# The second feed-forward norm turn of a two-block transformer kernel, taken by token halves around the last down product

## The reference, cut to what matters

```python
    # first block, per layer
        u = causal_dwconv(hn @ w_up[l], conv_w[l], conv_b[l])
        gate, val = jnp.split(u, 2, axis=-1)
        f = (jax.nn.gelu(gate, approximate=True) * val) @ w_down[l]
        h = h + rms_norm(f, ln_ffn_post[l])
    # second block
        h = rms_norm_2(x, norm1[l])
        proj = h @ w_in[l]

def rms_norm(x, g, eps=NORM_EPS):
    x32 = x.astype(jnp.float32)
    y = x32 * lax.rsqrt(jnp.mean(x32 * x32, axis=-1, keepdims=True) + eps)
    return (y * g.astype(jnp.float32)).astype(x.dtype)
```

## Time and profile before

| | us |
|---|---|
| median of 3 runs | 2956.19 (2954.12 to 2957.56) |
| the profiled execution, own time | 2959.0 |
| its span | 2957.2 |
| PE busy | 2835.6 |
| DVE, ACT, POOL busy | 1848.0, 1269.7, 623.0 |

### The profile page before, as it was taken

How to read it: one execution, slowest core, us unless ns; L and a number is a source line. 1 busy time by engine, 2 the same in 40 slices (tenths; PEclk the granted TensorE clock), 3 DMA queues, 4 the chain that set the end, 5 groups by cost and what they waited for, 6 DMA issues and landing times.

```text
span 2957.2 us, 47458 instructions
## 1 busy us (share of the span) xinstructions
PE 2835.6 (96%) x19678; PEld 2274.4 (77%) x19678; DVE 1848.0 (62%) x2351; ACT 1269.7 (43%) x1879; POOL 623.0 (21%) x313
## 2 busy tenths in 40 slices
PE   8999998889899999999899999999899999999999
PEld 6877777777688888788678867766578888888887
DVE  3157778852599999866685554565645766653446
ACT  4145555542554555443543433343433423333334
POOL 4310122221100000254151200000012122245443
PEclk9999999999999999999999999999899999999999
DMA  6443330002423333465544553435544344465664
GB/s 216 151 121 114 110 131 30 27 26 79 143 89 106 102 101 107 155 220 180 175 133 153 164 178 122 129 112 160 192 150 131 115 150 145 150 216 196 211 238 171
DMA packets 306280, 413.79 MB, mean 140 GB/s; under 512 B 13569, under 2 KB 189834, under 8 KB 306066
## 3 DMA queue, kind: packets, MB, share of 16 engines
q1 hardware_dynamic: 291090, 363.56, 38.6%
q10 hardware_dynamic: 14976, 47.19, 4.2%
HBM read 280.64 MB, written 130.06 MB: 139 GB/s over the span
## 4 chain that ended last, share of the span: by engine, by line
PE 80%; DVE 8%; DMA 4%; issue 3%; ACT 3%; SPq 1%; POOL 1%; DVEq 0%; ACTq 0%; POOLq 0%
PE ps L511 17%; PE ps L2767 16%; PE ps L3300 13%; PE ps L3082 10%; PE ps L2124 5%; PE ps L695 4%; PE ps L1544 4%; PE ps L2175 2%; PE ps L2194 2%; DVE cb L3385 2%; PE ps L2152 1%; PE ps L1607 1%; PE ps L2155 1%; DMA kl<-qk_lo 1%; DMA residual<-src 1%
## 5 line engine op out<-in xcount | busy, mean ns | idle before, releaser
L477 POOL TENSOR_TENSOR wl<-wraw,wh 128x1024 fp32r<-128x1024 f32 x62 | 157.4, 2538 | 1103.0 <-ACT wh L472 1093.4
L511 PE MATMUL ps<-xh,wh 128*128 128x512 f32 x752 | 237.9, 398 | 5.2 <-POOL wl L477 2.3
L511 PE MATMUL ps<-xl,wh 128*128 128x512 f32 x752 | 233.3, 392 | 0.0
L511 PE MATMUL ps<-xh,wl 128*128 128x512 f32 x752 | 232.9, 391 | 0.0
L472 ACT ACTIVATE wh<-wraw 128x1024 fp32r<-128x1024 f32 x78 | 82.4, 1056 | 266.0 <-PE ps L511 205.3
L2756 POOL TENSOR_TENSOR h_dl<-h_dr,h_dh 128x1024 fp32r<-128x1024 f32 x36 | 94.7, 2633 | 477.8 <-ACT h_dh L2738 477.6
L511 PEld LDWEIGHTS ps<-xh,wh 128*128 128x128 f32 x752 | 139.6, 189 | 46.7 <-issue 9.0
L2767 PE MATMUL ps<-h_dh,h_fh 128*128 128x512 f32 x448 | 174.8, 390 | 0.7 <-POOL h_dl L2756 0.7
L2767 PE MATMUL ps<-h_dh,h_fl 128*128 128x512 f32 x448 | 174.4, 389 | 0.0
L2767 PE MATMUL ps<-h_dl,h_fh 128*128 128x512 f32 x448 | 174.3, 389 | 0.0
L511 PEld LDWEIGHTS ps<-xl,wh 128*128 128x128 f32 x752 | 142.4, 189 | 30.3
(11 more groups left out here) (507 smaller groups left out, 7634.6 us busy)
## 6 DMA issues: line engine op xcount, KB each, us to landing
h_fr<-act_d SPq DMA_DIRECT2D x60, 512.0 KB, 3.9
act_d<-act SPq DMA_DIRECT2D x16, 1792.0 KB, 6.7
wraw<-in_w_in SPq DMA_DIRECT2D x48, 512.0 KB, 5.0
h_dr<-in_w_down SPq DMA_DIRECT2D x44, 512.0 KB, 4.8
r_raw<-in_w_up SPq DMA_DIRECT2D x38, 512.0 KB, 3.9
residual<-src ACTq DMA_DIRECT2D x32, 512.0 KB, 5.1
w_raw<-in_w_up SPq DMA_DIRECT2D x32, 512.0 KB, 5.1
l_fr<-act_d SPq DMA_DIRECT2D x31, 512.0 KB, 3.9
```

Source lines behind the costliest of these rows:

```text
L477: nc.gpsimd.tensor_tensor(wl[:, s, :, :], wraw[:, s, :, :], wh[:, s, :, :].bitcast(F32), ALU.subtract).then_inc(w_lo, 1)
L511: mm = nc.tensor.matmul(ps[:, bank + h, :], w, x[:, h * HALF:(h + 1) * HALF], start=start and k == 0, stop=stop and k == 2)
```

## The change

Nothing that is computed changes, but the order and the widths do. A token half is 512 tokens (`FIRST`, `SECOND`).

- **Step 2's parts** are made by ACT between the convolution copies of the gate and the value half, by DVE between the taps of the two.
- **P4's homes.** Steps 36 to 41 use three homes of their own in place of four, in memory that the kept weights held. The first three loads wait for P6 and for sums of P7; the loads of 39 to 41 wait for PE's step i-3.
- **Second half.** Its squares and their sum are made around steps 36 and 37 (`second_half_squares_act`, `second_half_sum_dve`), PE's sum lies in the middle of step 37, the root and reciprocal behind, PE's spread in the middle of step 38. Then its eight tiles are normed, rounded, squared and stored in halves (`second_half_dve`, `second_half_act`): tiles 0 and 1 between the parts of steps 39 and 40, tiles 2 and 3 between those of 40 and 41, tiles 4 to 7 behind. Its residual tiles are loaded apart, one of these loads ahead of the load of step 41.
- **PE** multiplies both input units for the second half behind the last down product (`second_half_products`), then for the first half tile by tile (`first_half_units`). The first half's statistics lie in between.
- Residual loads and stores of this turn are 32 of 256 KB in place of 16 of 512 KB.

```diff
             ff1_tap(act, FF_TILES - 1, "g")
+            down_hi_act(act, down1, 2)
             ff1_tap(act, FF_TILES - 1, "v")
-            down_hi_act(act, down1, 2)
...
+            second_half_root_act(act)
+            down_hi_act(act, down1, LAST1 + 3)
+            for kt in (0, 1):
+                second_half_act(act, kt)
+            down_hi_act(act, down1, LAST1 + 4)
+            for kt in (2, 3):
+                second_half_act(act, kt)
+            down_hi_act(act, down1, LAST1 + 5)
+            for kt in (4, 5):
+                second_half_act(act, kt)
+            for m in (4, 5):
+                first_half_squares_act(act, m)
+            second_half_act(act, 6)
+            for m in (6, 7):
+                first_half_squares_act(act, m)
+            stat_root_act(act, 3, ROWS[0], HALF_BANK)
+            second_half_act(act, 7)
+            post_norm_act(act, 1, 16, 32, "norm1_2", FIRST)
...
-                down_products(pe, down1, i)
+                down_products(pe, down1, i, {LAST1 + 1: second_half_sums_pe, LAST1 + 2: second_half_spread_pe}.get(i))
             down_last_products(pe, down1)
-            post_sums_pe(pe, 24, KT - 2)
-            spread_pe(pe, 3)
-            paced_units(pe, U_FA, 0, 16, 32, 4)
+            second_half_products(pe, 0, 1, {2: lambda pe: first_half_sums_pe(pe, 24), 6: first_half_spread_pe})
+            second_half_products(pe, 1, 3, {})
+            first_half_units(pe)
...
+        def second_half_dve(dve, kt):
+            s = kt % 2
+            if kt == 0:
+                h1_pe.wait(dve, "spread", 0)
+            h1_dve.done(nc.vector.tensor_tensor(y[:, kt, SECOND], y[:, kt, SECOND], ps[:, 7, :], ALU.mult), f"m{kt}")
+            h1_dve.wait(dve, f"m{kt}", 0)
+            dve.wait_ge(h_loaded[s], 16 * (4 + kt // 2 + 1))
+            dve.wait_ge(src_stored[s], 16 * ((16 + kt) // 2))
+            h1_dve.done(nc.vector.scalar_tensor_tensor(
+                out=src[:, s, SECOND], in0=y[:, kt, SECOND], scalar=col("ln_ffn_post", kt), in1=hres[:, s, SECOND],
+                op0=ALU.mult, op1=ALU.add), f"r{kt}")
+            h1_act.wait(dve, f"x{kt}", 0)
+            h1_dve.done(nc.vector.scalar_tensor_tensor(
+                out=xl[:, kt, SECOND], in0=src[:, s, SECOND], scalar=col("norm1_2", kt),
+                in1=xh[:, kt, SECOND].bitcast(F32), op0=ALU.mult, op1=ALU.subtract), f"l{kt}")
+
+        def second_half_act(act, kt):
+            tile = src[:, kt % 2, SECOND]
+            h1_dve.wait(act, f"r{kt}", 0)
+            h1_act.done(nc.scalar.activation(xh[:, kt, SECOND], tile, ACT.Identity, scale=col("norm1_2", kt)), f"x{kt}")
+            nc.scalar.activation(y[:, kt, SECOND], tile, ACT.Identity, scale=col("norm1_2", kt))
+            h1_act.done(nc.scalar.activation(sq1[:, kt, FIRST], tile, ACT.Square), f"s{kt}")
+            act.dma_start(residual[kt][:, SECOND], tile).then_inc(src_stored[kt % 2], 16)
+
+        def second_half_products(pe, u, bank, after):
+            for kt in range(KT):
+                h1_dve.wait(pe, f"l{kt}", 0)
+                if u == 0:
+                    h1_act.wait(pe, f"s{kt}", 0)
+                    for q in (2, 3):
+                        mm = nc.tensor.matmul(ps[QUARTERS[q], STAT_BANK, 0:T // 4], ones[:, :],
+                                              sq1[:, kt, (q - 2) * T // 4:(q - 1) * T // 4], start=kt == 0, stop=kt == KT - 1)
+                    h1_pe.done(mm, f"p{kt}")
+...
+                half_tile(bank, u, kt, SECOND)
+                if kt in after:
+                    after[kt](pe)
+
+        def half_tile(bank, u, kt, part):
+            for w, x, k in ((wh, xh, 0), (wh, xl, 1), (wl, xh, 2)):
+                mm = nc.tensor.matmul(ps[:, bank, :], w[:, u, kt, :], x[:, kt, part],
+                                      start=kt == 0 and k == 0, stop=kt == KT - 1 and k == 2)
+            return mm
+
+        def first_half_units(pe):
+            for kt in range(KT):
+                square_sum_pe(pe, 32 + kt, (0, 1))
+...
+                pe.wait_ge(x_lo, 16 + kt + 1)
+                mm = half_tile(0, 0, kt, FIRST)
+                if 1 <= kt < KT - 1:
+                    half_tile(2, 1, kt - 1, FIRST)
+            mm.then_inc(mm_done, 1)
+            half_tile(2, 1, 6, FIRST)
+            spread_pe(pe, 4)
+            half_tile(2, 1, 7, FIRST).then_inc(mm_done, 1)
...
             for i in range(8, len(down1.steps)):
+                if i == LAST1 + 3:
+                    for kt in (0, 1):
+                        second_half_loads(sp, kt)
+                elif i == LAST1 + 5:
+                    second_half_loads(sp, 2)
                 down_load(sp, down1, i)
...
+        LAST1, TURNS = (d.steps.index(("P4", 0)) for d in downs)
```

More of the change, by code:

```diff
@@ L130 @@
     kept2: list
+    last: list
 CHUNK = 64
@@ L568, in spread_pe, with spread_half_pe @@
             mm.then_inc(spread_done, 1)
+        def spread_half_pe(of, half):
+            rows = ROWS[half]
+            for w, part in ((spread_even, 0), (spread_odd, 1)):
+                mm = nc.tensor.matmul(ps[:, 6 + half, part * T // 4:(part + 1) * T // 4], w[rows, :], of[rows, :],
+                                      start=True, stop=True)
+            return mm
         def rstd_copy_act(act, k):
@@ L2567, in build_program @@
         act2_stored = [sem(f"act2_stored{s}") for s in range(2)]
+        h1_act = Steps(sem("h1_act"), [f"q{m}" for m in range(KT)] + ["root"] +
+                       [f"{x}{kt}" for kt in range(KT) for x in "xs"])
+        h1_dve = Steps(sem("h1_dve"), [f"a{m}" for m in range(KT)] + ["rec"] +
+                       [f"{x}{kt}" for kt in range(KT) for x in "mrl"])
+        h1_pe = Steps(sem("h1_pe"), ["sum", "spread"] + [f"p{kt}" for kt in range(KT)])
         s1_dve = Steps(sem("s1_dve"), ["T1", "T3", "T2", "T4"])
@@ L2636, in post_norm_loads, with second_half_squares_act @@
                     sp.wait_ge(added, KT * k + kt - 1)
-                sp.dma_start(hres[:, kt % 2, :], residual[kt]).then_inc(h_loaded[kt % 2], 16)
+                elif k:
+                    h1_dve.wait(sp, f"r{KT - 2 + kt}", 0)
+                sp.dma_start(hres[:, kt % 2, part], residual[kt][:, part]).then_inc(h_loaded[kt % 2], 16)
+        def second_half_squares_act(act, m):
+            if m < 4:
+                act.wait_ge(down_added, down_added_by(down1, "P3", m))
+            else:
+                act.wait_ge(down_added, down_added_by(down1, "P7", m - 4))
+            if m >= 2:
+                h1_dve.wait(act, f"a{m - 2}", 0)
+            h1_act.done(nc.scalar.activation(sq[:, m % 2, SECOND], y[:, m, SECOND], ACT.Square), f"q{m}")
@@ new lines, in second_half_sum_dve, with second_half_sums_pe @@
+        def second_half_sum_dve(dve, m):
+            h1_act.wait(dve, f"q{m}", 0)
+            if m == 0:
+                dve.wait_ge(stat_root, 3)
+                ins = nc.vector.tensor_copy(ss[:, SECOND], sq[:, 0, SECOND])
+            else:
+                h1_dve.wait(dve, f"a{m - 1}", 0)
+                ins = nc.vector.tensor_tensor(ss[:, SECOND], ss[:, SECOND], sq[:, m % 2, SECOND], ALU.add)
+            h1_dve.done(ins, f"a{m}")
+        def second_half_sums_pe(pe):
+            pe.wait_ge(down_added, down_added_by(down1, "P3"))
+            h1_dve.wait(pe, f"a{KT - 1}", 0)
+            h1_pe.done(quarter_sums(ss, True, True, (2, 3)), "sum")
@@ new lines, in second_half_root_act, with second_half_reciprocal_dve, second_half_spread_pe @@
+        def second_half_root_act(act):
+            h1_pe.wait(act, "sum", 0)
+            rows = ROWS[1]
+            h1_act.done(nc.scalar.activation(root1[rows, :], ps[rows, STAT_BANK, 0:T // 4], ACT.Sqrt,
+                                             bias=small[rows, 0:1], scale=1.0 / D), "root")
+        def second_half_reciprocal_dve(dve):
+            h1_act.wait(dve, "root", 0)
+            h1_dve.done(nc.vector.reciprocal(root1[ROWS[1], :], root1[ROWS[1], :]), "rec")
+        def second_half_spread_pe(pe):
+            h1_dve.wait(pe, "rec", 0)
+            h1_pe.done(spread_half_pe(root1, 1), "spread")
@@ L2640, in down_home @@
         def down_home(d, i):
+            name, c = d.steps[i]
+            if name == "P4" and d.last:
+                return d.last[c % 3]
             return (d.later if d.later and i >= 4 else d.homes)[i % 4]
@@ L2781, in down_products @@
             for b in range(4):
+                if b == 2 and half_way is not None:
+                    half_way(pe)
                 if c == 0 and name in DOWN_BEFORE:
@@ L3518, in _ @@
                     load_w(sp, U_QKV2, 1, w_cols(a["w_in_2"], 0))
-            sp.wait_ge(down_done, down_done_by(down1, down1.steps.index(("P4", 3))))
-            post_norm_loads(sp, 1)
+            for kt in range(3, KT):
+                second_half_loads(sp, kt)
+            post_norm_loads(sp, 1, FIRST)
             sp.wait_ge(x_lo, 17)
@@ L4202, in _ @@
                     ff1_taps(dve, t, x)
-                    if not more and x == "v":
```

(3 more changed lines are left out.)

223 lines of the change are left out of this document (142 added, 81 removed).

## The result

The changed kernel takes 2971.36 us (median of 6 runs, 2962.32 to 2973.44) beside 2955.12 for the kernel before: ratio 1.0047, 95% interval 1.0037 to 1.0058. It is 16 us slower where I forecast 4, and lies above my range, which ended at 2967. The profiled execution took 2973.44 us, its span is 2971.7 (before 2957.2).

A forecast was written before the change was run, and what follows sets the result against it. PE, busy 96% of the span, was taken as the bound. The seam's 5.6 us longer less the first place's 1.4 made +4.2 on 2956.2: 2960.4 us, range 2951.5 to 2967.

The forecast's parts named there:

- the stall: PE standing between step 39 and joint steps 40 and 41, until POOL's part of step 41: 11.3 us, ends 9 and 13.
- the price of the statistics calls: PE's calls summing squares for the norm: four quarters 0.57 us, two quarters taken as 0.30, ends 0.23 and 0.57.
- The seam: Step 36's first product to the next input unit's first: forecast 5.6 us longer, 58.6 against 53.0 in the stretch summed.
- sums and spread in steps 37, 38, and gaps to the stall: Added PE work in the down steps: two sums in step 37 (0.3) and a spread in 38 (0.5), +0.8 us.
- joint steps and clock: Steps 40 and 41 on PE, 8.2 us, plus 2.0 for the lower clock behind the stall (0 to 3.0).
- unit one, second half, with sums, spread, wait for tile 7: PE behind the joint steps: products and calls 8.3, first half's sums 0.9, spread 0.5, wait for tile 7 0.9 us.
- first half: PE's products of both units with statistics calls, tile by tile: 12.8 us, with 0.4 for late tiles 13.2.
- tail: First unit's end to next unit's start: 7.0 us, ends 5.2 and 8, last release by DVE's bank reading (`fa`).
- The spread: PE's spread of the first half's root, behind unit one's second half: 0.5 us.
- C: Rival: transfers bind the first half, residual sums needing the store two tiles before; +7.6 us, 2968.0; chance 0.18.
- A: Rival: the filling works, PE finds steps 40 and 41 ready; -9.1 us, 2947.1; chance 0.10.
- The first place: Around steps 2 and 3, near 1239.89: PE stands 1.0 and 4.1 us instead of 5.28; gain 1.4, bounds 0.4 and 3.4.

The follow-up runs named there:

- e5: Changed kernel with the eight statistics calls of unit one's second half in different shapes (one, two or four quarters, 128 or 256 tokens); single run, 2967.49 us.
- e7: Changed kernel with the second half's eight statistics calls in two groups of four, before tile 3's and tile 7's products of unit one; 2966.82 us.
- e1: Kernel before with only step 2's parts moved between the gate and value taps; 2957.88 us, ratio 1.0008 to before.
- e2: Changed kernel with step 2's parts put back behind the value taps, so the seam change stands alone; 2971.51 us, ratio 1.0053 to before.
- e9: e6 with the second half's squares kept and summed in the first half's four-quarter calls, last norm tile's products and first half's spread moved; 2962.95 us.
- e10: Changed kernel with the second half's squares kept and summed in the first half's four-quarter calls, none in unit one's second half; 2967.26 us.
- e6: Changed kernel with parts of steps 40 and 41 earlier, DVE's norm tiles interleaved, copies of blocks 0 and 1 before tile 5; 2963.91 us.

## Why the prediction was wrong, point by point

The direction and the stall were right; the price of the statistics calls was wrong, in its rule as well as in its size. The seam's ledger, forecast against the profile after:

| Piece | Forecast | Measured |
|---|---|---|
| sums and spread in steps 37, 38, and gaps to the stall | 0.8 | 2.1 |
| stall before the joint steps | 11.3 | 10.25 |
| joint steps and clock | 8.2 + 2.0 | 10.2 |
| unit one, second half, with sums, spread, wait for tile 7 | 10.6 | 13.4 |
| unit two, second half | 5.5 | 5.5 |
| first half | 13.2 | 15.9 |
| tail | 7.0 | 5.8 |
| sum | 58.6 | 63.2 |

(Measured: 1414.66 + 22.0 for four steps = 1436.7, PE stands from 1438.8 to 1449.02, joint steps to 1459.23, unit one to 1472.64, unit two to 1478.18, first half to 1494.1, tail to 1499.88.)

**The step that failed** is "for two quarters I take 0.30, with 0.23 and 0.57 as ends". A call takes 0.56 us itself, the upper end, and the first product behind it takes 0.2 more, which no end held. Against my 1.04 and 1.09 us for the first unit's share of a tile, both halves take 1.45: 0.41 x 8 + 0.36 x 8 = 6.2 us, more than the 2.8 + 2.7 in the table, since two waits that I had put in, 0.9 for tile 7 and 0.4 for late tiles, did not come. I had the earlier trace rows, where four quarters cost 0.57, and halved it; nothing in the trace said that the price follows the number of quarters. The Trainium skill, TensorEngine Tiling (Array Packing), section "Key Properties", says that tiles of the array work in parallel and that a change of tiling mode drains the engine; the first half of that is what e5 measures (1.46 and 1.44 us), the second fits the fixed part, which e7 saves with each change taken away (0.34 us), though no run here separates a drain from what else changes between the two kinds of matmul. That rule spoke against the change, and I had not weighed it.

**The spread** was the same error: with the sums in step 37 it makes the 2.1 in the first line of the ledger, and it comes again in unit one. The PE timeline after has the half spread and what follows it, and the product behind the second norm's full spread (which starts at 1495.53, above):

```profile
1470.23 0.70 PE L587 MATMUL ps<-root,spread_even 64*128 64x256 f32 x2
...
1471.28 0.62 PE L2756 MATMUL ps<-sq,ones 128*32 128x256 f32 x4
...
1496.60 0.49 PE L2775 MATMUL ps<-xh,wh 128*128 128x512 f32 x1
```

The half takes 1.05 us and the full one 1.07; I had put half the price, 0.5, for the half.

**Steps that held.** The stall by the queue, 10.25 for 11.3 (0.5 of the difference is a wait of tile 0 for POOL's step 39, which had ended before), with tile 2's residual sum at 2.12 us beside POOL's operation, and low clock behind it. That this sum waits for POOL like the taps (the Trainium skill, SBUF — State Buffer, section "SBUF: two separate sides") agrees with the row: 0.75 us alone, 2.12 when POOL runs. The first half ran without a break of PE, so C was rightly not the forecast, though with 3.8 us a store its condition was met. A is out by the stall.

**The first place** came as worked out in its shape (0 and 3.37 us of stalls for 1.0 and 4.1, clock 0.74), but DVE's last sum for step 7's input now met a POOL operation (2.75 us), the store and the load behind it came later, and PE waited 0.27 us for step 7 at 1268.07. I had not followed the work that far. Of the gain of 1.4 that I took off, the two profiles show 0.7 here and 1.2 in e1; the times of e1 and e2 show none.

**The tail**: 5.8, not 7.0, and the last release was POOL's, not `fa`. I had put POOL first and DVE's long sum behind it. The sum took its 2.23 us without a wait, and it was POOL's subtraction that grew, ending 0.8 us behind `fa`:

```profile
1495.30 4.52 POOL L480 TENSOR_TENSOR wl<-wraw,wh 128x1024 fp32r<-128x1024 f32 x1 [46.42 <-ACT wh L475]
```

In e9 and e10 it is `fa` that comes last.

**What is left over.** The forecast missed 4.7 us in the seam, 0.7 in the first place (by the profile), and 0.6 in front of the seam: step 36 needs an add of P7 by DVE, and DVE had square sums queued ahead of it, which I had counted as idle time. The half-clock stretch behind the seam added 1.1. So the change accounts for 10.3 + 0.6 - 0.7 = 10.2 us, 11.3 with that stretch; of a loss of 14 to 16 us that leaves 3 to 5. Half-clock stretches elsewhere move a run by as much (the one at 2354 alone is 3.2); whether some of it belongs to the change is open.

**Where the idea's gain went.** Before, PE stood for 9.7 of the 53 us. The split doubles the calls (8 more at 0.77, 6.2 us) and adds a spread (1.3 in the stream); the two sets of sums take 1.6 us together, as the one set did. That is an estimate of 7.5 us of PE work, and the windows of the seam show 6.5 (71.66 for 65.20). Even e6, with 3.25 us of stall, is 3.1 us longer in the seam than the kernel before, and e9, which has the eight calls for nothing, meets the stores. No version here beats the kernel before; that none could is argued, not shown.

## What to carry to other kernels

Before halving a piece of work to fill a gap, price the halves from a row of the same shape; where the quarters of the array run side by side, as here, half a call costs a whole one, and a split doubles its price. Then count what the split adds on the busiest engine against the gap itself: here 6.5 to 7.5 against 9.7 us, before any new wait. And when parts of a later step are woven into a chain of dependent tiles, look for the queue behind the first: taking away the 10 us wait brought a 2 us one, and lightening PE brought out the stores.
